# One half of the tokens: two products of the first chunks run together, tile by tile, and its transposes go in pairs

## What is computed

```
def rms_norm(x, g):
    xf = x.astype(jnp.float32)
    y = xf * lax.rsqrt(jnp.mean(xf * xf, axis=-1, keepdims=True) + EPS)
    return (y * g.astype(jnp.float32)).astype(x.dtype)
...
def hybrid_mixer(h, w_in, ...):
    z = h @ w_in
    (aq, ak, av, iq, ik, iw, pin, gu, gv, sq, sk, sv, gl) = jnp.split(z, _split_points(), axis=-1)
    ... four mixers on these parts, merged by gates, one output projection ...

def reference(x, ...):
    for l in range(DEPTH):
        h = rms_norm(x, mix_norm[l])
        x = x + hybrid_mixer(h, w_in[l], ...)
        h = rms_norm(x, ffn_norm[l])
        x = x + swiglu_ffn(h, w_ffn_gate[l], w_ffn_up[l], w_ffn_down[l])
    return x
```

## Time and profile before

| | us |
|---|---|
| median of 3 runs (753.31 to 753.86) | 753.76 |
| time of the profiled execution | 753.66 |
| span of its trace | 751.9 |
| TensorE busy | 746.8 |
| VectorE busy | 613.8 |
| ScalarE busy | 413.5 |

### The profile page before, as it was taken

The page is one execution under the profiler, slowest core; times in us unless marked ns, Lnnn a source line. Parts: engine busy times, 40 slices in busy tenths (PEclk is TensorE's granted clock), DMA queues, the critical chain, the costliest instruction groups (busy, mean ns, idle before and its releaser), DMA issues.

```text
span 751.9 us, 11619 instructions
## 1 busy us (share of the span) xinstructions
PE 746.8 (99%) x4542; PEld 661.6 (88%) x4542; DVE 613.8 (82%) x835; ACT 413.5 (55%) x639; POOL 123.7 (16%) x140
## 2 busy tenths in 40 slices
PE   8999999999999999999999999999999999999998
PEld 8988888988888888779888899999889999999887
DVE  6645988878788976695999899889989888888991
ACT  6654545456663655465449656556544556656430
POOL 6200050457303121741330000000000000000000
PEclk9999999999999999999999999999999999999999
DMA  8381213231133223415526635335073333339202
GB/s 282 102 243 43 70 57 113 64 105 57 57 112 102 67 71 98 165 59 171 138 98 172 179 117 164 114 110 199 4 259 108 111 112 111 113 112 324 69 29 84
DMA packets 67878, 89.55 MB, mean 119 GB/s; under 512 B 3108, under 2 KB 52592, under 8 KB 67696
## 3 DMA queue, kind: packets, MB, share of 16 engines
q1 hardware_dynamic: 65696, 84.55, 34.6%
q0 software_dynamic: 1984, 4.14, 2.8%
q10 hardware_dynamic: 144, 0.13, 0.1%
HBM read 81.99 MB, written 4.19 MB: 115 GB/s over the span
## 4 chain that ended last, share of the span: by engine, by line
PE 98%; DMA 1%; DVE 0%; ACT 0%; issue 0%; SPq 0%; DVEq 0%
PE bank L2531 14%; PE bank L2532 14%; PE bank L2533 14%; PE bank L2862 9%; PE bank L2861 9%; PE bank L2863 9%; PE bank L3044 5%; PE bank L3048 5%; PE bank L3046 5%; PE bank L2954 2%; PE bank L2955 2%; PE bank L2956 2%; PE bank L2986 1%; PE bank L2987 1%; PE bank L2985 1%; PE bank L2746 1%
## 5 line engine op out<-in xcount | busy, mean ns | idle before, releaser
L2531 PE MATMUL bank<-h_hi,w_hi 128*128 128x512 f32 (+1 forms) x336 | 128.5, 382 | 0.0
L2533 PE MATMUL bank<-h_hi,w_lo 128*128 128x512 f32 (+1 forms) x336 | 127.5, 379 | 0.0
L2532 PE MATMUL bank<-h_lo,w_hi 128*128 128x512 f32 (+1 forms) x336 | 127.4, 379 | 0.0
L2861 PE MATMUL bank<-t_hi,w_hi 128*128 128x256 f32 x320 | 88.4, 276 | 0.0
L2863 PE MATMUL bank<-t_hi,w_lo 128*128 128x256 f32 x320 | 88.3, 276 | 0.0
L2862 PE MATMUL bank<-t_lo,w_hi 128*128 128x256 f32 x320 | 88.3, 276 | 0.0
L1647 DVE TENSOR_TENSOR w_lo<-raw,w_hi 128x2048 fp32r<-128x2048 f32 x26 | 62.8, 2417 | 14.0 <-ACT w_hi L983 12.5
L2533 PEld LDWEIGHTS bank<-h_hi,w_lo 128*128 128x128 f32 x336 | 63.2, 188 | 12.1
L2531 PEld LDWEIGHTS bank<-h_hi,w_hi 128*128 128x128 f32 x336 | 63.2, 188 | 11.9 <-issue 0.3
L2532 PEld LDWEIGHTS bank<-h_lo,w_hi 128*128 128x128 f32 x336 | 63.2, 188 | 11.4
L2862 PE MATMUL bank<-f_lo,w_hi 128*128 128x256 f32 x240 | 66.3, 276 | 0.0
(11 more groups left out here) (419 smaller groups left out, 1918.8 us busy)
## 6 DMA issues: line engine op xcount, KB each, us to landing
raw<-in_w_in_dram SPq DMA_DIRECT2D x26, 1024.0 KB, 5.1
raw<-in_w_ffn_up_dram SPq DMA_DIRECT2D x11, 1024.0 KB, 5.2
raw<-in_w_ffn_gate_dram SPq DMA_DIRECT2D x10, 1024.0 KB, 5.1
raw<-in_w_ffn_down_dram SPq DMA_DIRECT2D x7, 1024.0 KB, 5.1
raw<-in_w_branch_dram SPq DMA_DIRECT2D x4, 1024.0 KB, 4.9
b<-in_w_ffn_down_dram SPq DMA_DIRECT2D x4, 1024.0 KB, 6.4
x_sb<-in_x_dram SPq DMA_DIRECT2D x6, 512.0 KB, 4.7
o<-in_w_out_dram SPq DMA_DIRECT2D x2, 1024.0 KB, 7.3
```

Of the source, the lines that this page charges most:

```text
L2531: mm(dst, l_hi, r_hi, start=start, stop=False)
L2532: mm(dst, l_hi, r_lo, start=False, stop=False)
L2533: return mm(dst, l_lo, r_hi, start=False, stop=stop)
L2861: mm(dst, l_hi, r_hi, start=begin and k == 0, stop=False, skip_group_check=True)
```

## The change

Only TensorE's program in `first_chunks` is written anew. The first half of the tokens keeps its order. In the last part of it (second product, j = 1), the pairs of transposes of the second half go two at a time: 0 and 1 after tile 4, 2 and 3 after tile 6, 4 after tile 7, where before 0, 1, 2 and 3 came one each after tiles 4, 5, 6 and 7, and 4 behind 3. In the second half, for each tile k the two matmuls of the first product are followed at once by the three of the second product's j = 0; j = 1 follows with all eight tiles as before. Pairs 5, 6 and 7 are issued ahead of tiles k = 0, 1 and 2 as before, but there are now five matmuls between them, and not two. The same matmuls and transposes are issued, with the same operands; each sum adds its terms in the same order.

```diff
+                def first_product(half, k):
...
+                def second_product(half, j, k):
...
+                for k in range(KT):
+                    second_product(0, 1, k)
+                    if k in (4, 6):
+                        turn_h(1, k - 4)
+                        turn_h(1, k - 3)
+                turn_h(1, 4)
+                for k in range(KT):
+                    pe.wait_ge(S["h_lo_ready"], KT + k + 1)
+                    if k + 5 < KT:
+                        turn_h(1, k + 5)
+                    first = first_product(1, k)
+                    if k == KT - 1:
+                        first.then_inc(filled, 1)
+                    last = second_product(1, 0, k)
+                last.then_inc(filled, 1)
+                for k in range(KT):
+                    last = second_product(1, 1, k)
+                last.then_inc(filled, 1)
```

More of the change, by code:

```diff
@@ L2633, in first_chunks @@
                 pe.wait_ge(S["first_lo"], 1)
-                for half in range(2):
+                def first_product(half, k):
                     cols = slice(half * SEQ // 2, (half + 1) * SEQ // 2)
[L2636 to L2667, removed]
@@ new lines, in first_product @@
+                    w = w_hi[:, k * P:(k + 1) * P]
+                    mm(bank[0][:, cols], w, h_hi[:, k, cols], start=k == 0, stop=False)
+                    return mm(bank[0][:, cols], w, h_lo[:, k, cols], start=False, stop=k == KT - 1)
+                def second_product(half, j, k):
+                    cols = slice(half * SEQ // 2, (half + 1) * SEQ // 2)
+                    w = slice(w_at(1) + k * CW + j * P, w_at(1) + k * CW + (j + 1) * P)
+                    return three(bank[1 + j][:, cols], w_hi[:, w], w_lo[:, w], h_hi[:, k, cols], h_lo[:, k, cols],
+                                 k == 0, k == KT - 1)
@@ new lines, in first_chunks @@
+                for k in range(KT):
+                    pe.wait_ge(S["h_lo_ready"], k + 1)
+                    if k + 5 < KT:
+                        turn_h(0, k + 5)
+                    if k == KT // 2:
+                        pe.wait_ge(hi_ready, 1)
+                        pe.wait_ge(lo_ready, 1)
+                    first_product(0, k)
+                for k in range(KT):
+                    for piece, (a, z) in enumerate(SECOND_LOWS):
+                        if a == k and z < KT:
+                            pe.wait_ge(S["second_hi"], (z + 1) // 2)
+                            pe.wait_ge(S["second_lo"], piece + 1)
+                        elif a == k:
+                            pe.wait_ge(hi_ready, 2)
+                            pe.wait_ge(lo_ready, 2)
+                    second_product(0, 0, k)
```

## The result

| | median, us | runs | lowest to highest |
|---|---|---|---|
| before | 753.69 | 6 | 753.31 to 754.41 |
| changed | 756.61 | 6 | 755.03 to 757.47 |

The changed kernel is slower, by about 0.35%: ratio 1.0035, 95% interval 1.0022 to 1.0048. The forecast was 754.4 us with a range up to 755.1, and it gave 92% to a change within 0.2%. The direction was right, the size was not. The profiled execution took 757.47 us with a span of 755.7, 3.8 us more than the span of before.

What follows compares the result with a forecast made beforehand. TensorE was taken as the bound, with no idle time from 30 us on. Removing a stall (-0.36 us) and adding a wait (+0.96) gave +0.6 on the median of 753.76: 754.4 us, range 753.2 to 755.1.

Steps and rivals of the forecast that it cites:

- The stall that is removed: TensorE's wait for DVE's low parts at tiles 5 to 7 of the second half goes: -0.36 us.
- case C: Second half: the old stall stays, but the new wait, ended by DVE, swallows it; 754.4 us, 80% together with the forecast.
- The pairs two at a time: Transposes of pairs 0 to 3 grouped by two cost TensorE the same: 0 at the end, bounds -0.1 and +0.1 us.
- Pair 7 is 0.72 us later: Transposes of pair 7 start at 22.84 instead of 22.12, so ACT's last high part starts 0.64 us later, at 23.26.
- rival A: Ahead of chunk 2 the new wait does not bind, leaving only the 0.36 us gain: 753.4 us, 12%.
- What is queued behind it on ACT: High parts of chunks 2 and 3 follow without pause, delaying DVE by 0.64 us; chunk 2 starts about +0.6 us later.
- TensorE has no time in which to get it back: Behind chunk 2's start TensorE has no idle time, so the whole 0.6 us reaches the end.
- Rival B: TensorE's clock falls to 1.2 GHz over the eight bank-alternating mixed tiles: +4.8 us, some 759.2 us in all, 3%.
- that stall (0.95 us): TensorE idle ahead of chunk 2, at 30.4 to 31.3; its new wait was summed as +0.96 us.
- The rule on cycling through banks: Cycling PSUM banks each iteration makes TensorE pause and its clock go up and down; the trace showed no instance.
- rival D: DVE's delay ahead of chunk 2 grows, for instance as iq_lo waits for ACT: at worst 1 us more, 755.4 us, 5%.

Runs made afterwards that it cites:

- one_tile: Kernel before, with only one tile (three matmuls) of the second product put ahead, behind the first product's tile 5 of the second half: 754.04 us, ratio 1.0000.
- only_pairs: Changed kernel with the second half's two products one behind the other as before; only the transposes go two pairs at a time: 753.94 us, ratio 0.9998.
- only_mixed: Changed kernel with the second half's transposes one pair at a time as before, the two products still mixed: 756.50 us, ratio 1.0027.
- after_moved: Changed kernel with chunk 0's weights in a buffer of their own, sharing no column with chunk 3: 754.44 us, ratio 1.0005.
- moved_early: Changed kernel with chunk 0's weights in their own buffer, and the second product's tiles 0 and 1 behind the first product's tile 2: 754.06 us, ratio 1.0004.
- before_late: Kernel before, with chunk 3's low part computed twice on DVE and no mixed tiles: 757.25 us, ratio 1.0042.

## Why the prediction was wrong, point by point

- *The stall that is removed, -0.36 us on TensorE.* Right as a reading of TensorE alone: mixed tiles at 0.60 us with no wait, and from the first product's first matmul to the transposes behind the second half 8.18 us (22.16 to 30.34 in the changed kernel) against 8.55 (21.34 to 29.89), 0.37 less. Worth nothing at the end, as one_tile shows; the prediction's case C had said that DVE's time swallows it.
- *The pairs two at a time, 0.* Right: only_pairs, 0.9998.
- *Pair 7 is 0.72 us later, ACT's last high part at 23.26, chunk 2's high part at 23.62.* Right: 23.25 and 23.62 in only_mixed. The traces of after_moved and moved_early show its worth, 0.6 us. With it rival A falls, which had ACT in time.
- *"What is queued behind it on ACT is the high parts of chunks 2 and 3 ... followed each other without a pause", so both move by 0.64.* **This step failed.** Chunk 3's high part waits for the first product as well. The change moves the first product's last matmul from 24.02 to 26.16 (only_mixed), and with it chunk 3's high part to 26.54, not 25.5. I took the absence of a pause in the trace for the absence of a dependency. The term should have been +1.3 us for chunk 2's start, and not +0.6. I had asked of the transposes how much later they stand, and not of the first product's end, which is the thing that the change moves most.
- *TensorE has no time in which to get it back, so the whole delay reaches the end.* Right: 2.16 + 1.60 us at chunk 2 is the 3.8 us of the span.
- *Rival B, the clock falls: 3%.* The clock fell in four runs of six, at another place and for another reason than the rival gave. In the mixed tiles it stayed at 1.00. The stall behind them lowered it. The prediction mentioned that stall (0.95 us) and then priced it at nothing but its length: a second term that was missing, worth 1.6 us in the profiled run. In after_moved, where that stall was 0.46 + 0.28 us by the trace, the clock held (1.000 in ten runs of eleven, 0.999 in one). At 1.16 + 0.28 us in the changed kernel it mostly did not. The rule on cycling through banks that the prediction quoted from the Trainium skill ("TensorE: Matmul & The Clock Gate", section "A second HAM failure mode: psum-queue depth-cycling") did not come into play.
- *The range, 753.2 to 755.1.* Its upper end had only small delays of DVE in it (rival D, 5%). It had no case for a delay whose cause the trace does not show, nor for a clock that multiplies a stall.

## What to carry to other kernels

When a step is moved later, list everything that waits for its end, from the program and not from the trace: a wait that was long met leaves no row, and a buffer used again for the next chunk's weights is such a wait. A stall is worth removing only if the engine behind it is not itself nearly late at the next meeting point; look there first. And a new stall on TensorE is to be priced as its length plus the chance that the clock falls behind it.

## What the runs showed of the hardware

Some 1.4 us of waiting on TensorE, in a stretch that otherwise held only small transposes, was enough to lower the granted clock in 8 of 11 runs (changed and only_mixed together), at a cost of 1.6 us in the profiled one; 0.7 us of waiting (after_moved) did not lower it in 11 runs, but for one at 0.999. In none of the three traces with a fall did it come during the wait: it came at 33.1 to 33.2 us, 0.2 us behind chunk 2's start in the changed kernel, 1.0 us behind it in only_mixed and 0.1 us behind it in before_late, and the upper level was back between 36.5 and 36.7. A look at the stall itself therefore shows a clock of 1.00. Why not every run falls is open. Twelve 128x128 transposes of an identity in the gap kept the clock up in 11 runs of 11, to 0.001. The second half of the input landed at a time that moved the middle of the trace by up to 0.8 us from one profiled execution to the next, so chunk 2's start is to be compared only after taking that off. That this is also what scatters the unprofiled runs is argued and not shown.
